# Ten RMSNorm square sums per token block on four 32-column tiles of TensorE, with a selector-matmul spread of rstd

## What is computed

```python
def rms_norm(x, g):
    xf = x.astype(jnp.float32)
    y = xf * lax.rsqrt(jnp.mean(xf * xf, axis=-1, keepdims=True) + EPS)
    return (y * g.astype(jnp.float32)).astype(x.dtype)
...
    x = x + 0.5 * rms_norm(swiglu(rms_norm(x, f1_pre), f1_wg, f1_wu, f1_wd), f1_post)
    h = rms_norm(x, m_pre)
    z = h @ w_in
...
    x = x + rms_norm(mix, m_post)
    x = x + 0.5 * rms_norm(swiglu(rms_norm(x, f2_pre), f2_wg, f2_wu, f2_wd), f2_post)
    gate = jax.nn.sigmoid(rms_norm(x, e_pre) @ e_wg)
    x = x + rms_norm(gate * (p @ e_wp), e_post)
```

## Time and profile before

| | us |
|---|---|
| median of 3 runs | 2665.72 |
| lowest, highest | 2664.89, 2725.86 |
| the profiled execution | 2664.45 |
| its span on the slowest core | 2662.7 |
| spans of the 8 cores | 2655.2 to 2662.7 |
| TensorE busy in the span | 2552.5 |

### The profile page before, as it was taken

How to read it: one execution, slowest core, us unless ns; L and a number is a source line. 1 busy time by engine, 2 the same in 40 slices (tenths; PEclk the granted TensorE clock), 3 DMA queues, 4 the chain that set the end, 5 groups by cost and what they waited for, 6 DMA issues and landing times.

```text
span 2662.7 us, 52925 instructions; the slowest of 8 cores (2655.2 to 2662.7 us)
## 1 busy us (share of the span) xinstructions
PE 2552.5 (96%) x18352; PEld 1677.8 (63%) x18576; DVE 1132.0 (43%) x2680; ACT 1090.5 (41%) x2220; POOL 613.8 (23%) x943
## 2 busy tenths in 40 slices
PE   6999999999999999999999999999989999999996
PEld 3676565666566666666566765667656676566764
DVE  2222775215621368321662137722174215772237
ACT  3123673125611376322741237722274124761236
POOL 0052232004305223100420412400051222240014
PEclk9999999999999999999999999999999999999998
DMA  8354252434335524233655542533343444334341
GB/s 164 58 94 82 41 96 49 75 66 83 53 76 91 93 43 89 48 70 66 124 124 96 114 89 37 93 64 65 63 80 64 83 70 83 42 72 80 61 83 65
DMA packets 54595, 205.43 MB, mean 77 GB/s; under 512 B 10656, under 2 KB 23744, under 8 KB 39456
## 3 DMA queue, kind: packets, MB, share of 16 engines
q0 software_dynamic: 32608, 178.81, 38.2%
q1 hardware_dynamic: 21728, 23.23, 3.1%
HBM read 372.17 MB, written 9.63 MB: 143 GB/s over the span
## 4 chain that ended last, share of the span: by engine, by line
PE 90%; DVE 3%; ACT 3%; issue 3%; DMA 1%; POOL 1%; DVEq 0%; SPq 0%; ACTq 0%; POOLq 0%
PE PS L614 88%; PE PS L620 2%; ACT L490 1%; DVE XT L656 1%; ACT SCR L645 1%; DVE R L663 0%; ACT SQS L645 0%; DMA RING<-W 0%; DMA XT<-xT 0%; DVE SCR L663 0%; POOL R L651 0%; DVE SCR L656 0%; ACT R L645 0%; ACT PS L645 0%; POOL XT L656 0%
## 5 line engine op out<-in xcount | busy, mean ns | idle before, releaser
L614 PE MATMUL PS<-R,RING 128*128 128x256 bf16 (+2 forms) x10439 | 1602.3, 310 | 52.0 <-ACT SCR L645 23.9
L614 PEld LDWEIGHTS PS<-R,RING 128*128 128x128 bf16 x10560 | 1030.7, 98 | 556.1 <-issue 75.2
L645 ACT ACTIVATE SCR<-PS 128x256 f32<-128x256 f32 (+2 forms) x818 | 372.3, 463 | 965.6 <-PE PS L614 948.9
L614 PE MATMUL PS<-HIDR,RING 128*128 128x256 bf16 (+2 forms) x4934 | 752.8, 309 | 10.0 <-ACT SQS L645 3.5
L656 DVE TENSOR_TENSOR HIDR<-SCR,PS 128x512 bf16<-128x512 f32 (+2 forms) x552 | 282.3, 512 | 873.2 <-PE PS L614 856.5
L614 PEld LDWEIGHTS PS<-HIDR,RING 128*128 128x128 bf16 x4992 | 487.4, 98 | 252.3 <-issue 3.3
L685 POOL DMA_DIRECT2D RING<-W x192 | 106.5, 555 | 1585.7 <-PE PS L614 1526.8
L645 ACT ACTIVATE SQS<-PS 128x256 bf16<-128x256 f32 (+2 forms) x288 | 131.4, 456 | 436.9 <-PE PS L614 432.6
L656 POOL TENSOR_TENSOR XT<-XT,SCR 128x256 f32<-128x256 f32 (+2 forms) x221 | 206.0, 941 | 270.1 <-DVE SCR L663 246.0
L663 DVE SCALAR_TENSOR_TENSOR R<-XT,VECT,PS 128x256 bf16<-128x256 f32 (+2 forms) x368 | 186.0, 564 | 65.7 <-ACT PS L645 53.2
L490 ACT ACT_TABLE_LOAD x163 | 209.1, 1283 | 2.9
(11 more groups left out here) (92 smaller groups left out, 1063.4 us busy)
## 6 DMA issues: line engine op xcount, KB each, us to landing
RING<-W POOLq DMA_DIRECT2D x116, 1024.0 KB, 8.6
RING<-W POOLq DMA_DIRECT2D x64, 704.0 KB, 6.1
RING<-W POOLq DMA_DIRECT2D x8, 768.0 KB, 6.5
XT<-xT SPq DMA_DIRECT2D x8, 512.0 KB, 10.9
XT<-xT SPq DMA_DIRECT2D x16, 256.0 KB, 9.0
yT<-SCR SPq DMA_DIRECT2D x16, 256.0 KB, 3.2
yT<-SCR SPq DMA_DIRECT2D x32, 128.0 KB, 2.2
RING<-W POOLq DMA_DIRECT2D x4, 512.0 KB, 5.1
```

The lines of the kernel that those rows point to most:

```text
L614: S.add("pe", lambda e: e.matmul(out.build(), lhsT.build(), rhs.build(), start=start, stop=stop), r=[lhsT, rhs], w=[out], dur=max(n, 64) / ...
L645: return e.activation(out=out.build(), in_=in_.build(), func=func, **k2)
```

## The change

The 480 square-sum matmuls become 480 groups of four (`stat4`). Each of the four takes a quarter of the tokens, w = n/4 columns, with only 32 columns of `ONESB` as the stationary operand, and writes 32 partitions of the bank, columns 0 to w: a quarter j lands on partitions 32j to 32j+31. The four lie on four 32-column tiles of the array. The mean squares of n tokens so stand in w columns.

`rstd4` takes Ln and Exp on w columns. It then splits the result into the upper 16 bits (`hi`, the bfloat16 made by cutting) and the rest (`lo`, a subtraction on VectorE), and spreads both over all partitions with 8 full-array matmuls of w columns: the stationary operand is one of four selector matrices (`SELB`), which picks the 32 partitions of quarter j with weight 1/32 and writes columns jw to (j+1)w. The six folded norms keep their old way.

```diff
+    SELB = sb("SELB", [128, 512], BF16)
...
+    MEMSET(SELB[:], 0.0)
+    for j in range(4):
+        MEMSET(SELB[32 * j:32 * j + 32, 128 * j:128 * j + 128], 1.0 / 32.0)
...
+        def stat4(st, src, n, first, last, prio, acq=()):
+            w = n // 4
+            MMB([(bv(st, 0, w, 32, 32 * j), fx(ONESB[:, 0:32]), src(j * w, j * w + w), first, last) for j in range(4)],
+                max(w, 78) / 2400.0 + 0.003, prio, acq=acq, tag="stat")
+
+        def rstd4(st, n, g, eps=EPS):
+            w = n // 4
+            t = Buf("scr")
+            a, b, r = bv(st, 0, w), bv(t, 0, w), bv(t, w, 2 * w)
+            hi = r.map(lambda x: x.bitcast(BF16).rearrange("p (n two) -> p n two", two=2)[:, :, 1])
+            lo = b.map(lambda x: x.bitcast(BF16)[:, 0:w])
+            ACT(b, a, AF.Ln, w, (0, g - 50), bias=eps, scale=1.0, acq=[t], tag="ln")
+            ACT(r, b, AF.Exp, w, (0, g - 50), scale=-0.5, sbuf=True, tag="exp")
+            TT_(lo, r, hi, ALU.subtract, w, (0, g - 50), tag="lo")
+            sel = [fx(SELB[:, 128 * j:128 * j + 128]) for j in range(4)]
+            out = [bv(st, j * w, j * w + w) for j in range(4)]
+            MMB([(out[j], sel[j], hi.map(lambda x: x), j == 0, False) for j in range(4)], 4 * (max(w, 100) / 2400.0 + 0.003), (0, g - 50), tag="bc")
+            MMB([(out[j], sel[j], lo.map(lambda x: x), False, j == 3) for j in range(4)], 4 * (max(w, 100) / 2400.0 + 0.003), (0, g - 50), tag="bc")
...
-                    MM(bv(st2, 0, n), fx(ONESB[:]), bv(sq, 0, n), n, k == 0, k == KC - 1, (0, g), acq=[st2] if k == 0 else (), tag="stat")
-                rstd_inplace(st2, n, g)
+                    stat4(st2, lambda a, b, sq=sq: bv(sq, a, b), n, k == 0, k == KC - 1, (0, g), acq=[st2] if k == 0 else ())
+                rstd4(st2, n, g)
...
-                MM(bv(self.st, 0, n), fx(ONESB[:]), bv(sq, 0, n), n, self.c == 0, self.c == KC - 1, (0, g),
-                   acq=[self.st] if self.c == 0 else (), tag="stat")
+                stat4(self.st, lambda a, b: bv(sq, a, b), n, self.c == 0, self.c == KC - 1, (0, g), acq=[self.st] if self.c == 0 else ())
+                self.quad = True
...
-            rstd_inplace(ys.st, n, g, eps)
+            (rstd4 if ys.quad else rstd_inplace)(ys.st, n, g, eps)
...
-                    MM(bv(st2, 0, n), fx(ONESB[:]), Hs(si, m), n, m == 0, m == KC - 1, (0, g), acq=[st2] if m == 0 else (), tag="stat")
+                    stat4(st2, lambda a, b, m=m: Hs(si, m, a, b), n, m == 0, m == KC - 1, (0, g), acq=[st2] if m == 0 else ())
...
-                rstd_inplace(st2, n, g)
+                rstd4(st2, n, g)
```

More of the change, by code:

```diff
@@ L850, in __init__ @@
             def __init__(self, si, g):
-                self.si, self.st, self.c, self.g = si, Buf("st"), 0, g
+                self.si, self.st, self.c, self.g, self.quad = si, Buf("st"), 0, g, False
             def fold(self, src, n, g):
```

## The result

| | us |
|---|---|
| changed kernel, first measurement, 6 runs | 2693.17 to 3061.69, median 2766.99 |
| before, in the same measurement, 6 runs | median 2666.49 |
| ratio to before | 1.0173, 95% interval 1.0129 to 1.0217 |
| changed kernel measured again beside the experiments, 6 runs | 2695.42 to 3110.49, median 2697.77 |
| before, there | median 2666.51 |

In many runs of either kernel some cores were granted a lower clock and the run took longer; the ratios leave such runs out except 2730.26 us in the first measurement and 2727.70 in the second (slowest cores at 0.974 and 0.977), and without these two the changed kernel takes 2693 to 2699 us, 27 to 32 us or 1.0 to 1.2% more than before. The forecast was 2711, within 2690 to 2742.

A forecast was written before the change was run, and what follows sets the result against it. TensorE's instruction stream was taken to bound the kernel; -70.3 + 18.9 + 7.6 + 18.6 + 69.6 + 7 - 5 = +46.4 us on 2664.45 gave 2710.9, predicted as 2711, range 2690 to 2742.

The forecast's parts named there:

- What bounds the kernel: Whole kernel: the length of TensorE's instruction stream sets the time; savings on ScalarE or VectorE are worth next to nothing.
- What goes, and the groups: Square sums on TensorE: 70.3 us of old matmuls go; groups of four cost 18.9 us plus 7.6 for starting tiles.
- the rival that denied it: Square-sum groups: the four 32-column tiles do not stream at once, +51.4 us, 2762 us; chance 0.08.
- The start of four tiles: Square-sum groups: starting four tiles costs 0.02 us in each of 380 stretches, 7.6 us.
- The rival with weight loads one behind the other: Square-sum groups: four weight loads follow one another, 0.08 us instead of 0.02 per stretch, +23 us, 2734; chance 0.10.
- The spread: After each rstd: 480 full-array matmuls that spread it over all partitions add 18.6 us to TensorE.
- The changes of form: TensorE between neighbouring matmuls of different tile shape: 733 more changes at 0.095 us each, +69.6 us.
- The rival of free changes: Tile-shape changes around groups: they cost nothing, since all groups use 128 rows; -32.8 us, 2632; chance 0.07.
- Waits: TensorE's waits: longer chains behind the last square sum add 7 us; a slower TensorE absorbs 5, bounds 0 and 15.
- The `lo` matmuls as a block: Spread in 60 norms: TensorE blocks on `lo` matmuls while the subtraction queues, 0.5 us each, +30 us, 2741; chance 0.07.
- the 20 that were to show the forecast wrong: Profile after the change: waits for VectorE's subtraction above 20 us would prove the forecast wrong.
- The sum: Whole kernel: all terms together add 46.4 us to the profiled 2664.45, giving 2710.9; predicted 2711.

The follow-up runs named there:

- four tiles with all tokens: Kernel before, each square-sum matmul made into four matmuls on 32-column tiles, each with all n columns; 2726.0 and 2726.87 us, ratio 1.0227.
- One quarter: Changed kernel, each group of four made one full-array matmul of w columns summing only the first quarter of the tokens; median 2647.08 us, ratio 0.9923.
- `no lo`: Changed kernel without the VectorE subtraction and four of the eight spread matmuls, so rstd has 16 bits; median 2679.43 us, ratio 1.0050.
- the batch: Changed kernel, 42 of 60 norms issuing their eight groups together behind the last square, other 18 as before the change; median 2664.66 us, ratio 0.9987.

## Why the prediction was right, and where its sizes were off

- *What bounds the kernel*: right. TensorE's stream sets the time; the 45 us less on ScalarE (26 were forecast) brought nothing that the account shows. All gains and losses are in the stream's small parts, beside 2380.3 us of weight matmuls.
- *What goes, and the groups*: forecast -70.3 + 18.9 + 7.6 = -43.8, measured -47.4 for the square sums and +3.1 of small excess, -44.3 together. The four tiles ran at once: the rival that denied it falls by the 0.24 us of a group of four and by the four tiles with all tokens. The start of four tiles was charged with 0.02 us for each of 380 stretches; it is 0.010 us for each of 480 groups, 4.8 us in all against 7.6. The rival with weight loads one behind the other asked for 0.08 us between first and last and falls too.
- *The spread*: 18.6 forecast, 18.4 measured.
- *The changes of form*: 69.6 forecast, 74.6 measured in the changed kernel and 75.1 alone. This step decides the sign. It was read from a few of the 32 round trips between other forms in the trace of before, and its 0.095 us for each nearly held over 733 more: 0.102, with 0.09 in and 0.10 to 0.11 out. The rival of free changes falls twice.
- *Waits*: this is the term that was mis-sized. I had put +7 for longer chains and -5 for waits that a slower TensorE absorbs, +2 in all; measured were -16.4. One quarter against the changed kernel shows that TensorE's slowness absorbed 29.5, beyond my bound of 15. One quarter against before shows +13.1 for order, chain and a stream 35 us shorter together. At the rate of the first comparison (29.5 us of waits for 80.4 of stream) the shorter stream alone would bring some 13 us, an estimate, and at that of the four tiles with all tokens (16.6 for 78.5) some 7; so order and chain brought between nothing and 6 us, about my +7 or less, and how much of it is each stays open. The four tiles with all tokens give 16.6 for absorption in the old order, just over the bound. I had read the waits of the earlier trace rows one by one as something that stays unless a cause goes. They are differences between two streams: each lone group delays TensorE by 0.04 to 0.13 us against before, just where norms are made, and the engines that make them run on. That this is how the waits shrink is argued, not shown; that they shrink is measured twice.
- *The `lo` matmuls as a block*: TensorE waits 2.0 us for the subtraction, far from the 20 that were to show the forecast wrong. The `no lo` kernel's waits fall by 2.6 us, by 5.7 with convolution and half clock. Its stream is 11 us shorter too, which at the rate above would bring some 4 us of waits back (an estimate), so up to 10 us may hang on `lo`, not 30.
- *The sum*: +46.4 forecast; +34.4 in the account, of which 2.2 are only moved behind Ln and Exp, and 27 to 32 us in the times. The waits came out 18 us lower than forecast, the changes of form 5 higher, convolution and half clock 2.5 higher. 2711 lies 12 to 18 us above the runs of 2693 to 2699. That it lies at the centre of the first interval (1.0173 x 2666.5 = 2713) is luck: that ratio rests on two runs, 2693.17 and 2730.26 us.

That the trace agreed with the Trainium skill's statement of a drain at a change of tiling mode (TensorEngine Tiling (Array Packing), Tiling Modes, Key Properties) is now measured by itself, 75.1 us for 740 changes. The estimate of 2744, worked out from the price of a weight load that the Trainium skill gives (TensorE: Matmul & The Clock Gate, LDWEIGHTS) for four loads in a row, did not come true: the four loads of a group are drawn as one stretch of 0.10 us, hardly longer than one load of 0.09, and the four matmuls start within 0.01 us.

## What to carry to other kernels

Price a change of array tile shape at 0.1 us each way before splitting a matmul over column tiles: a lone group of four gains nothing below some 650 columns (an estimate: 0.20 us, the 0.26 of a group less its columns, over three quarters of n at 0.42 ns a column; the widest run here had 512), so batch the groups until a stretch saves more than its two changes. If the engine that sets the time gets slower, part of its waits are absorbed, and if it gets faster they return, so test a part by taking it out and reading the waits too. And what is saved in the stream can be given back in waits and at half clock: here the batch saved 15.6 us of stream and gained nothing clear of noise, and it paid only in the version with one step taken out of the chain behind the last input.

## What the runs showed that I had not expected

Waits moved by 30 us (77.0 to 106.5) with all other engines' instructions and their order unchanged, by no more than TensorE's own 80 us. Four column tiles with all columns cost 3.4 us more over 480 groups than one full-array matmul each (0.6 in the square sums, 2.8 in the small excess), their changes of form left aside. And a plan with prices near the measured ones made a kernel slower by 9 us than one whose price for a group of 128 columns (0.056 us) was less than a quarter of the measured 0.26.
